# A hybrid encoder layer on one Trainium2 core: three late queries moved in the order of slots, merges shifted, the end of the lookups handed over row by row

## The reference

```python
n = rms_norm(h, norm1_g[l]) * (1.0 + scale1) + shift1
y = hybrid_mixer(n, ...)          # three mixers, gated and merged, times w_out
h = h + gate1 * y
n = rms_norm(h, norm2_g[l]) * (1.0 + scale2) + shift2
h = h + gate2 * peer_ffn(n, peer_wq[l], peer_subkeys[l], peer_u[l], peer_v[l])

# peer_ffn, per block of 128 tokens
q = (xb @ w_pq).reshape(TOKEN_BLOCK, PEER_HEADS, 2, PEER_QDIM // 2)
s = jnp.einsum('nhpd,hpkd->nhpk', q, sub_keys)
# top 16 of 128 on each side, top 16 of the 256 sums: expert (n,h,16), g = softmax(best_s)
u, vv = u_tab[expert], v_tab[expert]
act = gelu(jnp.einsum('nd,nhkd->nhk', xb, u))
return jnp.einsum('nhk,nhkd->nd', g * act, vv)
```

## Time and profile before

| | |
|---|---|
| median of 3 runs | 2041.88 us (2039.61 to 2043.86) |
| the profiled execution, its own time | 2041.46 us |
| its span, first to last instruction | 2039.7 us |
| PE busy | 1670.9 us, 82% |
| DVE busy | 1443.5 us, 71% |
| ACT busy | 579.5 us, 28% |
| POOL busy | 632.1 us, 31% |
| read from HBM | 655.52 MB, of which gathers 536.90 MB |
| granted TensorE clock, mean | 0.910 |
| first gather issued | 614.2 us |
| last gather issued | 2001.4 us |

### The profile page before, as it was taken

One profiled execution on the slowest core, in us unless ns is written; L12 is line 12 of the kernel. 1 busy time (PEld: TensorE's weight loads), 2 busy tenths in 40 slices (PEclk: granted clock), 3 DMA queues, 4 the chain that ended last, 5 costly groups with the idle time before them and its releaser, 6 DMA issues.

```text
span 2039.7 us, 17878 instructions
## 1 busy us (share of the span) xinstructions
PE 1670.9 (82%) x5626; PEld 946.5 (46%) x5626; DVE 1443.5 (71%) x3353; ACT 579.5 (28%) x1272; POOL 632.1 (31%) x542
## 2 busy tenths in 40 slices
PE   4999989999998898999888867777877676667676
PEld 3533446667786565556555523334433222222222
DVE  5353642668328788887778899878777878887876
ACT  2111114664224253442211223222222222222221
POOL 0000001110003433334333545444444544445441
PEclk8999998999999999999899978878898988888888
DMA  9633020221449999999999999999999999999995
GB/s 375 250 131 118 7 88 10 77 93 57 163 177 372 385 419 419 401 398 406 406 420 420 419 417 405 421 419 419 420 420 421 420 419 420 420 419 419 420 419 228
DMA packets 89183, 659.79 MB, mean 323 GB/s; under 512 B 9968, under 2 KB 10240, under 8 KB 15488
## 3 DMA queue, kind: packets, MB, share of 16 engines
q0 software_dynamic: 73728, 536.90, 63.9%
q1 hardware_dynamic: 14768, 120.75, 15.0%
q10 hardware_dynamic: 592, 0.98, 0.1%
HBM read 655.52 MB, written 2.82 MB: 323 GB/s over the span
## 4 chain that ended last, share of the span: by engine, by line
PE 41%; DMA 34%; DVE 12%; issue 7%; ACT 4%; POOL 2%; SPq 0%; DVEq 0%; POOLq 0%; PEldq 0%; ACTq 0%
DMA sb<-uv_table,sb 33%; PE ps L1121 11%; PE ps L663 6%; PE ps L665 4%; PE ps L770 3%; PE ps L984 3%; DVE sb L2071 2%; DVE sb L2095 2%; POOL sb L2238 2%; PE ps L1023 2%; PE ps L1028 2%; PE ps L784 1%; PE ps L949 1%; DMA sb<-w_mod 1%; PE ps L1047 1%
## 5 line engine op out<-in xcount | busy, mean ns | idle before, releaser
L1121 PE MATMUL ps<-sb 128*128 128x512 f32 x1424 | 774.1, 689 | 273.0 <-ACT sb L1515 269.3
L2238 POOL DMA_INDIRECT sb<-uv_table,sb x512 | 605.1, 1182 | 870.9 <-PE ps L1121 657.4
L2071 DVE CUSTOM_DVE_ANT_0 sb<-sb 128x1024 f32<-128x1024 f32 x512 | 625.2, 1221 | 248.1 <-DMA sb<-uv_table,sb 240.1
L1121 PEld LDWEIGHTS ps<-sb 128*128 128x128 f32 x1424 | 292.3, 217 | 695.2 <-ACT sb L1515 392.0
L1515 ACT ACTIVATE sb<-sb 128x128 f32<-128x128 f32 x356 | 132.0, 397 | 607.1 <-DVE sb L2080 602.1
L2095 DVE SCALAR_TENSOR_TENSOR sb<-sb 128x512 f32<-128x512 f32 x304 | 214.7, 748 | 2.2
L1504 ACT ACTIVATE sb<-sb 128x2 f32<-128x2 f32 x256 | 51.7, 202 | 396.3 <-DVE sb L2071 396.2
L2200 POOL TENSOR_TENSOR sb<-sb 128x128 f32<-128x128 f32 x8 | 13.1, 1636 | 422.8 <-DVE sb L1776 422.8
L663 PE MATMUL ps<-sb 128*128 128x512 f32 (+1 forms) x304 | 125.2, 563 | 0.1
L984 PE MATMUL ps<-sb 128*128 128x256 f32 (+1 forms) x576 | 117.8, 359 | 0.3 <-issue 0.3
L984 PEld LDWEIGHTS ps<-sb 128*128 128x128 f32 x576 | 100.5, 197 | 30.8 <-issue 20.4
(11 more groups left out here) (281 smaller groups left out, 1776.7 us busy)
## 6 DMA issues: line engine op xcount, KB each, us to landing
sb<-w_mod SPq DMA_DIRECT2D x11, 2048.0 KB, 9.6
sb<-w_pq SPq DMA_DIRECT2D x18, 1152.0 KB
sb<-w_merge SPq DMA_DIRECT2D x24, 768.0 KB
sb<-w_proj SPq DMA_DIRECT2D x8, 2048.0 KB, 8.9
sb<-w_merge SPq DMA_DIRECT2D x6, 2304.0 KB, 9.0
sb<-w_out SPq DMA_DIRECT2D x8, 1024.0 KB, 10.5
sb<-uv_table,sb POOLq DMA_INDIRECT x512, 27.7
sb<-w_merge SPq DMA_DIRECT2D x3, 1536.0 KB, 6.5
```

The source lines that it names most:

```text
L1121: mm = pe.matmul(bank(2 * (t % 2) + f), dgw[m % NDG], row_v(n)[:, T * f:T * (f + 1)], start=(i == 0), stop=(i == PH * PK - 2))
L2071: dve.tensor_tensor_reduce(out=row_u(n), in0=row_u(n), in1=n2_tm(u // PH), scale=1.0, scalar=0.0, op0=ALU.mult, op1=ALU.add, accum_out=dot ...
L2238: pool.indirect_dma_start(out=ring[PLACE[n]], out_offset=None, in_=uv_table, in_offset=bass.IndirectOffsetOnAxis(ap=experts[u % 4][:, i:i ...
```

## The change

It has two parts. In the slots, queries 8, 9 and 10 go from slots 21, 25 and 44 to 42, 46 and 50; the first merge leaves slot 4 and all up to the ninth come one place later in the list, with slots 21 and 25 new and 4 and 29 gone; the late query of slot 2 goes to slot 3. The weights of queries 9 and 10 are loaded in the slots in which the scores of the query before them are made, so these two loads move from slots 23 and 27 to 44 and 48. At the end, the rows that DVE weighs in the last unit are 2, 5, 8 and 10 instead of 6, 9, 12 and 15; the last two lookups get gelu, weight and diagonal each by itself; DVE multiplies its own sum by the gate and adds the residual before the last two dots; and the last tile is finished and stored in two halves.

```diff
-        ON_DVE, ALSO_DVE = (6, 9, 12, 15), (1, 3)
+        ON_DVE, ALSO_DVE, LAST_DVE = (6, 9, 12, 15), (1, 3), (2, 5, 8, 10)
@@ on_dve
+            if u == NU - 1:
+                return i in LAST_DVE
@@
-        QUERY_SLOT = {(44 if q == 10 else 4 * (q - 3) + 1): q for q in range(3, 11)}
+        QUERY_SLOT = {(4 * q + 10 if q >= 8 else 4 * (q - 3) + 1): q for q in range(3, 11)}
@@ MERGE_SLOT
-            [4, 7, 8, 11, 12, 15, 16, 19, 20, 22, 23, 24, 26, 27, 28, 29, 30, 31, 32, 33, 34, 35, 36, 37])}
+            [7, 8, 11, 12, 15, 16, 19, 20, 21, 22, 23, 24, 25, 26, 27, 28, 30, 31, 32, 33, 34, 35, 36, 37])}
@@
-        LATE_QUERY_AT = {2: 2, 4: 3}
+        LATE_QUERY_AT = {3: 2, 4: 3}
@@ sync, the stores
-            for t in range(TT):
+            for t in range(TT - 1):
                 sp.wait_ge(s["added"], t + 1)
                 sp.dma_start(out[P * t:P * (t + 1), :], h_tm(t)).then_inc(s["stored"], 16)
-            sp.wait_ge(s["stored"], 16 * TT)
+            for f in range(2):
+                sp.wait_ge(s["added"], TT + f)
+                sp.dma_start(out[P * (TT - 1):T, T * f:T * (f + 1)], h_tm(TT - 1)[:, T * f:T * (f + 1)]).then_inc(s["stored"], 16)
+            sp.wait_ge(s["stored"], 16 * (TT + 1))
@@ tensor, query
-                    if q == 10:
-                        pe.wait_ge(s["yg_ready"], 8)
+                    if q == 8:
+                        pe.wait_ge(s["yg_ready"], 7)
@@ tensor, output_piece
-                    pe.wait_ge(s["q_out"], 10)
-                    pe.wait_ge(s["sc_out"], 10)
+                    pe.wait_ge(s["q_out"], 8)
+                    pe.wait_ge(s["sc_out"], 8)
@@ tensor, weigh
-                                   start=(i == 0), stop=(i == PH * PK - 2))
+                                   start=(i == 0), stop=(i == PH * PK - (2 if t < TT - 1 else 1)))
@@ scalar
+            def last_one(n):
+                i = n % PK
+                act.wait_ge(s["dot_done"], n + 1)
+                act.activation(gelu[(NU - 1) % 2][:, i:i + 1], dots[(NU - 1) % 2][:, i:i + 1], ACT.Gelu).then_inc(s["gelu_ready"], 1)
+                m = by_pe(n)
+                act.wait_ge(s["weighed"], m - NDG + 1)
+                act.wait_ge(s["w_ready"], NL // 2 + n - (NL - 2))
+                act.activation(dgw[m % NDG], ident, ACT.Copy, scale=wgt[(NU - 1) % 2][:, i:i + 1]).then_inc(s["dg_ready"], 1)
...
-                for pair in range(max(EARLY // 2, 2 * slot), 2 * slot + 2):
+                for pair in range(max(EARLY // 2, 2 * slot), min(2 * slot + 2, NL // 2 - 1)):
...
+            last_one(NL - 2)
+            last_one(NL - 1)
@@ vector
+            def weight_one(n):
+                i = slice(n % PK, n % PK + 1)
+                dve.wait_ge(s["gelu_ready"], NL // 2 + n - (NL - 2))
+                dve.tensor_tensor(wgt[(NU - 1) % 2][:, i], gelu[(NU - 1) % 2][:, i], share[(NU - 1) % 4][:, i], ALU.mult)\
+                   .then_inc(s["w_ready"], 1)
+            def own_part():
+                dve.wait_ge(s["dve_weighed"], by_dve(NL))
+                for f in range(2):
+                    ins = dve.tensor_tensor(acc_tmp[:, T * f:T * (f + 1)], acc_v[f], g2row[:, T * f:T * (f + 1)], ALU.mult)
+                done(ins)
+            def own_rest():
+                dve.wait_ge(s["tm_out"], 12)
+                done(dve.tensor_tensor(acc_tmp, acc_tmp, h_tm(TT - 1), ALU.add))
+            def finish_last():
+                t = TT - 1
+                dve.wait_ge(s["weighed"], by_pe(NL))
+                for f in range(2):
+                    dve.tensor_tensor(acc_v[f], bank(2 * (t % 2) + f), g2row[:, T * f:T * (f + 1)], ALU.mult).then_inc(v_step, 1)
+                v_count[0] += 2
+                for f in range(2):
+                    half = slice(T * f, T * (f + 1))
+                    dve.wait_ge(v_step, v_count[0] - 1 + f)
+                    dve.tensor_tensor(h_tm(t)[:, half], acc_v[f], acc_tmp[:, half], ALU.add).then_inc(s["added"], 1)
@@ vector, for n in range(NL)
+                if n == NL - 1:
+                    weight_one(NL - 2)
                 if n >= EARLY:
                     dot(n)
...
+                if n == NL - 3:
+                    own_part()
+                if n == NL - 2:
+                    own_rest()
...
-            weights(NL // 2 - 1)
-            weigh(NL - 1)
-            finish(TT - 1)
+            weight_one(NL - 1)
+            finish_last()
```

## The result

Over 22 runs each the changed kernel took 2046.28 us (2041.58 to 2050.96) and the kernel before 2040.56 us (2038.50 to 2045.46): ratio 1.0025, 95% interval 1.0019 to 1.0032. It is slower, by 5 to 6 us, where 2037.6 was forecast; the range (2031 to 2044) did not hold the time. Medians in this document are over all executions of a kernel; the ratios leave out four far slower ones (2251 to 3192 us, one each of slots_only and late_query_only, two of queries_only).

A forecast was written before the change was run, and what follows sets the result against it. Lookups bound by a gather stream near 420 GB/s, where only holes count; tail separate. Terms -3.6 - 1.7 + 1.0 - 1.9 + 0.9 + 1.3 = -4.0 us gave 2037.6 us, range 2031 to 2044.

The forecast's parts named there:

- The frame: Lookup stage: bytes are conserved, so only holes in the stream can be gained or made; the tail is its own chain.
- Slots 2 to 4, -3.6 us: Late query placed behind slot 2's rows: gathers 16 to 19 go sooner, gaining 3.6 of the 4.2 us hole at 660 to 675.
- the late weights: Slot 4: PE may wait 0 to 2.5 us for the last late query's weights; taken as 0, other end +3.
- Slots 20 to 29, -1.7 + 1.0: PE relieved, so the hole of 955 to 965 closes, -1.7 us; slot 21's heavier load is charged +1.0.
- the slower rival: Slots 20 to 28: merges in a row make PE wait on DVE, seven further holes; +7.6 there, 2047.7 us total, chance 0.14.
- the new merge of slot 21: Slot 21 carries 5.5 us where 2.05 stood, ahead of rows 84 to 87; charged +1.0 us, between 0 and 3.5.
- The loads, no term: Two query weight loads move later at 2.8 us each; saved early and paid later, so no term.
- Slots 42 to 52, -1.9 + 0.9: Moved loads fill the hole of 1255 to 1270, -1.9 us (other end 0); DVE's waits for scores cost +0.9.
- query 8's first half: Slot 42: it joins the last output piece on PE and hides in 4.38 us of idle at 1156.69; no charge.
- The waits for scores: Slots 42 to 52: DVE waits some 0.9 us three times before choosing; 0 to 2.7 us, +0.9 taken.
- The tail, +1.3: Last lookups and store: +0.6 us at full clock plus 0.7 for PE's clock; ends 0 and +7.8.
- The rival of the clock: Tail: PE's last four rows start and stay at 1.2 GHz; stage -5.3, tail +7.8, 2044 us; chance 0.08.

The follow-up runs named there:

- slots_only: Kernel before with the three slot moves (queries, merges, late query) and the old tail: 2046.84 us, ratio 1.0018.
- late_query_only: Kernel before with only the late query moved from slot 2 to 3: 2041.48 us, ratio 1.0002.
- queries_only: Kernel before with only queries 8, 9 and 10 moved to slots 42, 46 and 50: 2044.83 us, ratio 1.0009.
- after again: Second profile of the unchanged changed kernel, span 2046.0 us; that run's median 2048.40 us, ratio 1.0021 against the kernel before.
- after: First profile of the changed kernel, one of its fastest executions: own time 2042.18 us, span 2040.2 us.
- merge_4_to_21: Kernel before with the merge of slot 4 moved to slot 21 and the late query of slot 2 to 3: 2042.44 us, ratio 1.0002.
- merges_only: Kernel before with the changed merge list and late query, queries where they were: 2046.47 us, ratio 1.0019.
- merges_back: Changed kernel with the old merge list put back; moved queries, late query and new tail stay: 2047.30 us, ratio 1.0021.
- tail_row_back: Kernel before with the new tail, but row 508 on DVE and DVE's part of the last sum after the last dot: 2041.82 us, ratio 0.9999.
- merge_29_to_25: Kernel before with only the merge of slot 29 moved to slot 25: 2045.26 us, ratio 1.0015.
- tail_only: Kernel before with only the change's new tail, old slots: 2041.85 us, ratio 1.0003.
- no_two_loads: Kernel before without the query weight loads of slots 23 and 27, queries 9 and 10 using query 8's weights: 2037.51 us, ratio 0.9974.

## Why the prediction was wrong, step by step

**The frame was right.** Only holes can be gained or made, and the tail is a chain of its own: the table of holes accounts for every kernel's stage to about 1 us, as it nearly must.

**Slots 2 to 4, -3.6 us: right where it was read, not kept.** POOL's wait shrank from 8.14 to 4.74, the stretch rose to 380 GB/s (336 in after again), and dot 17 came 8.0 us earlier in after, 1.4 of it from the start of dot 0. Of this 4.9 us stood at dot 68 and 3.1 at dot 92; in after again dot 92 came 0.4 us later than before. Over 630 to 860 the holes went from 6.7 us to 4.9 in after and 7.0 in after again. PE's wait of 3.34 us for the late weights, which I set to 0 because the merge had left, came with the gather wait of 8.41 us behind it, and 690 to 715 lost bytes instead. The term was mis-sized where it began: I let the weights land within 6.5 us, and they took 8.5 and 9.8. merge_4_to_21, which has these edits and only one of the two added merges, gained nothing in the median.

**Slots 20 to 29, -1.7 + 1.0: this step failed.** I let the hole of 955 to 965 close, because PE is relieved. The hole grew: 925 to 1000 lost 6.1 us in after, 6.3 in after again, 7.1 in merges_only, 5.2 in queries_only, against 2.0 before. And in the changed kernel PE was not relieved: 9.4 us of queries leave, but 11.0 us of merges come in, by the prediction's own figures. From 860 to 1000 PE was busy 126.1 us in after and 123.6 in after again, against 124.4 before. Where PE was relieved (120.1 us in queries_only, 122.2 in merges_back), the hole grew all the same (5.2 and 5.0 us). So PE's busy time does not set it.

What the rows show is an order in PE's queue: a merge's second half waits for DVE's half merge, which stands behind the last dot of the slot before, and the rows of the slot stand behind the merge. A row that waits there keeps a place of the ring, and POOL waits for the place (13.04 us). This is the mechanism of the slower rival, and it is argued from the rows, not shown: the length of PE's wait does not go with the loss. tail_row_back, with the old slots, had 6.39 us of it and late_query_only 4.91, and the two lost 1.4 and 0.2 us between 925 and 1000. PE in tail_row_back:

```profile
987.96 3.39 PE L1033 MATMUL ps<-sb 128*128 128x256 f32 x8 [6.39 <-DVE sb L1935]
```

I charged the new merge of slot 21; by merge_4_to_21 and merge_29_to_25 the merge of slot 25 is the likelier cost. The slower rival's price, +7.6 us for a hole in every slot, was too high: one or two holes of 2 to 4 us, not seven. I gave it 0.14 because four merges in a row had made one hole only, and that hole was the very place to which the change added one.

**The loads, no term: right.** 2.8 us a load was borne out three ways: 5.7, 6.8 and 5.3 to 6.4 us for two.

**Slots 42 to 52, -1.9 + 0.9: the first failed, the second came.** The moved loads found no hole: dots 172 to 204 took 87.7 and 88.5 us instead of 81.8, and queries_only 87.5. 1250 to 1300 lost 1.0 and 1.4 us instead of 1.8. Slot 42 got a hole of its own, and the forecast had no term for it: 1100 to 1160 lost 1.9 to 2.9 us in all five profiles with moved queries (400 to 407 GB/s) and at most 0.2 in those without (419 or 420). I had written that query 8's first half hides in the 4.38 us of idle at 1156.69; it stands ahead of the last output piece, some 20 us earlier in PE's order, where there is no idle, and in after it waited 1.58 us there for ACT besides. The waits for scores came as forecast, 0.81 us three times; what of these 2.4 us reached the end is not to be told from the rest (0.9 was charged).

**The tail, +1.3: about right, and its other end real.** At full clock it is +0.3 (after, tail_only, merges_back), up to +0.4 against the other profiles with the old tail; forecast 0.6. At the clock of after again it is +2.0. I had charged 0.7 for the clock on top; between the executions it is 0 or 1.7. The rival of the clock was right in kind: the fall to half rate came inside the burst, after a pause, but did not last. The Trainium skill (TensorE: Matmul & The Clock Gate, "Why this matters for your kernels") says that longer pauses between matmul bursts cost the full rate. Both traces agree with it: in after again the fall follows PE's pause of 3.15 us; in after the clock fell to 0.5 (2024 to 2026) behind a pause of 3.00 us and was back at 1.0 when the burst began, ahead of which PE stood only 1.52 us. What the prediction could not know is which rows such a fall hits.

For the store, the Trainium skill (DMA: Bandwidth & Descriptors, "Anatomy of one DMA") gives a fixed 2.0 us plus the bytes at 436 GB/s, for the transfers that POOL issues; this store is issued by SP. The part for the bytes fits: 256 KB landed in 2.1 us and 512 KB in 2.7, a saving of 0.6 where I had taken 0.4 from the rows. The whole does not: an estimate by the figures of the Trainium skill is 2.6 and 3.2 us.

**The sum.** Forecast: stage -5.3, tail +1.3. Measured in the two profiles: stage +1.6 and +5.8, tail +0.3 and +2.0. By the table of holes, after and after again against before:

| stretch | forecast | after | after again |
|---|---|---|---|
| 630 to 860 | -3.6 | -1.8 | +0.3 |
| 860 to 1100 | -1.7 + 1.0 | +3.0 | +3.3 |
| 1100 to 1300 | -1.9 + 0.9 | +1.0 | +1.9 |
| sum | -5.3 | +2.2 | +5.5 |

The largest miss, 3.7 and 4.0 us, is that of slots 20 to 29; the early gain that did not last makes 1.8 and 3.9, slots 42 to 52 make 2.0 and 2.9.

**Open.** Why the hole of 925 to 1000 grows when only the queries leave (queries_only, 5.2 us), while it shrinks when only their loads leave (no_two_loads, 416 GB/s, 0.7 us), is not settled. That the order of the handshake makes this hole was not tested: no run moved the half merge in DVE's queue, or the rows ahead of a merge's second half in PE's. A place for query 8's first half behind the last output piece was not run either.

## What to carry to other kernels

Where a stream is full, price a move by the holes it closes and opens, not by the busy time it takes from an engine. Add up what comes into an engine's stretch as well as what leaves it. And a relieved engine closes a hole only if the hole came from its work (queries_only); look also at which handshake its work waits behind, in queue order. And look for idle time at the exact place in the queue where the moved step will stand, not at the nearest idle in time.
